# Attention by pairs: scores as three single-pass products of high and low parts, split a query tile at a time inside the stage

## The reference, cut to what matters

```python
# block one: 8 heads, one shared k, the picked keys, causal
logits = jnp.einsum('bthd,btkd->bthk', qb, k_sel).astype(jnp.float32) * (dh ** -0.5)
...
# layers: window_gqa, 6 heads, 2 kv heads, |i - j| <= 128, a sink logit per head
s = jnp.einsum('bnqkgd,bnjkd->bnkgqj', qb, kb).astype(jnp.float32) * (HEAD_DIM ** -0.5)
...
# layers: neighbourhood_attention, 4 heads, a window of 8 x 16 grid cells with a bias table
s = s + bias[None].astype(jnp.float32)
p = jax.nn.softmax(s.reshape(B, NA_HEADS, GRID_W, wh * ww), axis=-1)
```

## Time and profile before

| what | us |
|---|---|
| median of 3 runs | 3905.65 (3900.75 to 3908.73) |
| the profiled execution's own time | 3905.73 |
| its span, first to last instruction | 3903.6 |
| `attend_pairs` in block one | from 437.5 to about 577 |
| `attend_pairs` in the first layer | from 1369.5 to about 1506, neighbourhood pairs from about 1437 |
| `attend_pairs` in the second layer | from about 2736 to 2873 |

### The profile page before, as it was taken

The page is one execution under the profiler, slowest core; times in us unless marked ns, Lnnn a source line. Parts: engine busy times, 40 slices in busy tenths (PEclk is TensorE's granted clock), DMA queues, the critical chain, the costliest instruction groups (busy, mean ns, idle before and its releaser), DMA issues. The chain is left out here.

```text
span 3903.6 us, 54426 instructions
## 1 busy us (share of the span) xinstructions
PE 3484.6 (89%) x18514; PEld 2596.8 (67%) x18514; DVE 2633.7 (67%) x4362; ACT 2047.5 (52%) x3302; POOL 381.4 (10%) x300
## 2 busy tenths in 40 slices
PE   7998989599919999999599999799999995999996
PEld 4444558477718855668488888688556685888884
DVE  1896764588853175664699999631756646999996
ACT  1672451288732165553377777421645532777774
POOL 0002100022141001000011111010010000111110
PEclk9899899699959999999799999899999997999998
DMA  3100002477252110003499999621100034999997
GB/s 115 46 1 3 1 21 100 178 292 296 96 205 73 33 29 23 28 1 125 180 368 393 381 381 383 236 70 33 29 23 28 1 120 181 367 388 382 381 386 275
DMA packets 122029, 649.26 MB, mean 166 GB/s; under 512 B 14064, under 2 KB 22512, under 8 KB 69872
## 3 DMA queue, kind: packets, MB, share of 16 engines
q1 hardware_dynamic: 101392, 572.36, 37.8%
q0 software_dynamic: 15984, 58.20, 5.2%
q10 hardware_dynamic: 4464, 16.25, 1.0%
HBM read 584.38 MB, written 62.39 MB: 166 GB/s over the span
## 5 line engine op out<-in xcount | busy, mean ns | idle before, releaser
L3262 DVE TENSOR_TENSOR low_ring<-mix,high_ring 128x2048 fp32r<-128x2048 f32 x256 | 576.9, 2285 | 41.3 <-ACT high_ring L3211 41.3
L3211 ACT ACTIVATE high_ring<-mix 128x2048 fp32r<-128x2048 f32 x256 | 477.1, 1931 | 80.3 <-PEq L125 80.3
L3150 PE MATMUL ps<-high_ring,x_high 128*128 128x512 f32 x1024 | 408.6, 399 | 10.8 <-DVE low_ring L3262 7.1
L3151 PE MATMUL ps<-low_ring,x_high 128*128 128x512 f32 x1024 | 400.0, 391 | 0.0
L3152 PE MATMUL ps<-high_ring,x_low 128*128 128x512 f32 x1024 | 399.9, 391 | 0.0
L3262 DVE TENSOR_TENSOR low_ring<-more_raw,high_ring 128x2048 fp32r<-128x2048 f32 x128 | 290.3, 2287 | 24.3 <-ACT high_ring L3211 24.3
L3211 ACT ACTIVATE high_ring<-more_raw 128x2048 fp32r<-128x2048 f32 x128 | 246.3, 1924 | 0.0
L3150 PEld LDWEIGHTS ps<-high_ring,x_high 128*128 128x128 f32 x1024 | 192.3, 188 | 73.2 <-DVE low_ring L3262 19.6
L3152 PEld LDWEIGHTS ps<-high_ring,x_low 128*128 128x128 f32 x1024 | 192.3, 188 | 41.0
L3151 PEld LDWEIGHTS ps<-low_ring,x_high 128*128 128x128 f32 x1024 | 192.5, 188 | 37.6
L2717 DVE TENSOR_TENSOR w_unit_low<-mix,w_unit_high 128x1024 fp32r<-128x1024 f32 x32 | 40.9, 1289 | 245.7 <-ACT w_unit_high L2643 245.7
(11 more groups left out here) (495 smaller groups left out, 8124.7 us busy)
## 6 DMA issues: line engine op xcount, KB each, us to landing
mix<-in_expert_units SPq DMA_DIRECT2D x256, 1024.0 KB, 8.0
more_raw<-in_expert_units SPq DMA_DIRECT2D x128, 1024.0 KB, 8.6
raw_experts<-in_expert_units SPq DMA_DIRECT2D x16, 3072.0 KB, 11.5
expert_out<-out ACTq DMA_DIRECT2D x31, 512.0 KB, 2.8
mix<-in_w_turned SPq DMA_DIRECT2D x20, 512.0 KB, 3.7
qk_body<-residual SPq DMA_DIRECT2D x16, 512.0 KB, 8.0
qk_tail<-in_w_out SPq DMA_DIRECT2D x8, 1024.0 KB, 8.3
mix<-residual SPq DMA_DIRECT2D x16, 512.0 KB, 3.3
```

Of the source, the lines that this page charges most:

```text
L3150: nc.tensor.matmul(ps[:, bank, :], left_high, high, start=first, stop=False)
L3151: nc.tensor.matmul(ps[:, bank, :], left_high, low, start=False, stop=False)
L3211: nc.scalar.activation(w_high[:, n % RING, :], raw[n % RAW_UNITS], ACT.Copy).then_inc(high_ready, 1)
L3262: nc.vector.tensor_tensor(w_low[:, n % RING, :], raw[n % RAW_UNITS], w_high[:, n % RING, :].bitcast(F32), ALU.subtract).then_inc(low_ready, 1)
```

## The change

`attend_pairs` gets a list `splits`. An entry is a place (the number of the pair behind which it stands, or -1 for ahead of everything) and a list of parts. For each part ACT copies the raw fp32 operand to an fp32r tile `high`, and DVE subtracts, which gives `low` as fp32r in the place of the raw operand. PE's `score` waits for the step that its pair needs and makes three matmuls per head and unit: high by high, high by low, low by high, the two heads in turn.

In block one there are eight steps, at max(4t - 6, -1) for query tile t: four chunks of q and one of k, 640 columns of 128 rows. In a layer, a tile step at max(3t - 6, -1) holds 256 + 128 columns of q and k and 256 more of the next tile's k (and 256 further ones in the first step; the last has 384 in all), and four more steps of 1024 columns stand behind pairs 4, 8, 12 and 16, for the neighbourhood. So the steps of tiles 0 and 1 stand ahead of everything, and behind pair 12 stand two. The maxima, exponentials, values and transposes are as before. The diff, cut to its core:

```diff
-def attend_pairs(book, ps, ident, pairs, scale, widest, tables=None):
+def attend_pairs(book, ps, ident, pairs, splits, scale, widest, tables=None):
...
-                    for i in range(2):
-                        last = nc.tensor.matmul(ps[:, 2 * (u % 2) + i, 0:cols.stop - cols.start],
-                                                pair["q"][i * HD:(i + 1) * HD, :], pair["k"][i][:, cols],
-                                                start=True, stop=True)
+                    pe.wait_ge(low_made, pair["splits"])
+                    for x, (left, right) in enumerate(((0, 0), (0, 1), (1, 0))):
+                        for i in range(2):
+                            last = nc.tensor.matmul(ps[:, 2 * (u % 2) + i, 0:cols.stop - cols.start],
+                                                    pair["q"][left][i * HD:(i + 1) * HD, :],
+                                                    pair["k"][i][right][:, cols], start=(x == 0), stop=(x == 2),
+                                                    skip_group_check=True)
                     last.then_inc(scores_full, 1)
...
@@ ACT
+            def split(behind):
+                for at, parts in splits:
+                    if at == behind:
+                        for raw, high, _ in parts:
+                            ins = nc.scalar.activation(high, raw, ACT.Copy)
+                        ins.then_inc(high_made, 1)
+
+            split(-1)
             exponentials(0)
             for p in range(N):
...
                 if p + 1 < N:
                     exponentials(p + 1)
+                split(p)
...
@@ DVE
+            def split(behind):
+                for n, (at, parts) in enumerate(splits):
+                    if at == behind:
+                        dve.wait_ge(high_made, n + 1)
+                        for raw, high, low in parts:
+                            ins = nc.vector.tensor_tensor(low, raw, high, ALU.subtract)
+                        ins.then_inc(low_made, 1)
+
+            split(-1)
             maxima(0)
             maxima(1)
...
                 if p >= 2:
                     write(p - 2)
+                split(p)
                 i = p - sums_from
...
@@ block_one
+            splits = [(max(4 * t - 6, -1), [(raw[:, 0:4, tile(t)], high[:, 0:4, tile(t)], raw_low[:, 0:4, tile(t)]),
+                                            (raw[:, 6, tile(t)], high[:, 4, tile(t)], raw_low[:, 6, tile(t)])])
+                      for t in range(T)]
...
@@ layer_two
+                for t in range(T):
+                    of = [(body[:, 4:6, tile(t)], high[:, 4:6, tile(t)], body_low[:, 4:6, tile(t)]),
+                          (tail[:, 0, tile(t)], high[:, 6, tile(t)], tail_low[:, 0, tile(t)])]
+                    for c in ((0, 1) if t == 0 else (t + 1,) if t + 1 < T else ()):
+                        of.append((tail[:, 1:3, tile(c)], high[:, 7:9, tile(c)], tail_low[:, 1:3, tile(c)]))
+                    steps.append((max(3 * t - 6, -1), of, t))
+                for m in range(4):
+                    steps.append((4 + 4 * m, [(body[:, m, :], high[:, m, :], body_low[:, m, :])], T + m))
+                steps = sorted(steps, key=lambda step: step[0])
```

More of the change, by code:

```diff
@@ L3330, in _, with neighbourhood_pairs @@
                 expert(EXPERTS - 1, True, False)
-def neighbourhood_pairs(qk, v, bias, bias_mid, out):
+def neighbourhood_pairs(qk, v, bias, bias_mid, out, splits):
     pairs = []
@@ L3357, in sparse_pairs, with window_pairs @@
         for j in range(HEADS // 2):
-            pairs.append(dict(q=raw[:, j, tile(t)], k=(raw[0:HD, 6, 0:keys], raw[HD:P, 6, 0:keys]), keys=keys,
-                              add=(mask, mask), values=(values, values), out=out[:, t, tile(j)], sink=None))
+            pairs.append(dict(q=[of[:, j, tile(t)] for of in q_parts],
+                              k=([of[0:HD, 0:keys] for of in k_parts], [of[HD:P, 0:keys] for of in k_parts]), keys=keys,
+                              add=(mask, mask), values=(values, values), out=out[:, t, tile(j)], sink=None,
+                              splits=t + 1))
     return pairs
-def window_pairs(qk, v, band, sink, out):
+def window_pairs(qk, v, band, sink, out, splits):
     pairs = []
@@ L3371, in window_pairs @@
             kv = [h // (SWA_HEADS // 2) for h in (2 * j, 2 * j + 1)]
[L3372 removed]
+            pairs.append(dict(q=[of[:, tile(t)] for of in qk[4 + j]],
+                              k=([of[0:HD, keys] for of in qk[7 + kv[0]]], [of[HD:P, keys] for of in qk[7 + kv[1]]]),
                               keys=(hi - lo + 1) * P, add=(add, add),
                               values=[[v[:, c, g * HD:(g + 1) * HD] for c in range(lo, hi + 1)] for g in kv],
[L3375 removed]
+                              out=out[:, t, 640 + j * P:640 + (j + 1) * P], sink=sink[:, 2 * j:2 * j + 2],
+                              splits=splits[t]))
     return pairs
@@ L3511, in layer_two @@
                 sums += [(bias[:, h, GRID_W:], bias[:, h, GRID_W:], outside[:, GRID_W:]) for h in range(NA_HEADS)]
-                window = window_pairs(qk, feats[:, :, 640:768], band, sink, mix)
-                nearest = neighbourhood_pairs(qk, feats[:, :, 0:256], bias, bias_mid, mix)
-                attend_pairs(book, ps, ident, window + nearest, HD ** -0.5, 5 * P, (transfers, sums, len(window)))
+                high = sb(near, "qk_high", [P, 9, S], F32R)
+                low = [body_low[:, m, :] for m in range(MLA_HEADS)] + [tail_low[:, m, :] for m in range(3)]
+                parts = [(high[:, m, :], low[m]) for m in range(9)]
+                steps = []
+                for t in range(T):
[7 more added lines that the diff above has]
+                steps = sorted(steps, key=lambda step: step[0])
+                position = {step[2]: n + 1 for n, step in enumerate(steps)}
+                window = window_pairs(parts, feats[:, :, 640:768], band, sink, mix, position)
+                nearest = neighbourhood_pairs(parts, feats[:, :, 0:256], bias, bias_mid, mix, len(steps))
+                attend_pairs(book, ps, ident, window + nearest, [step[0:2] for step in steps], HD ** -0.5, 5 * P,
+                             (transfers, sums, len(window)))
             with ExitStack() as part:
```

25 lines of the change are left out of this document (19 added, 6 removed).

## The result

| what | before | the change |
|---|---|---|
| median, us | 3908.16 (20 runs, 3900.75 to 3911.97) | 3913.99 (20 runs; 19 of them 3907.27 to 3919.16) |
| ratio, 95% interval | | 1.0018 (1.0012 to 1.0024) |
| profiled execution's own time | 3905.73 | 3914.4 |
| its span | 3903.6 | 3912.6 |
| PE busy, DVE busy | 3484.6, 2633.7 | 3471.3, 2664.1 |

One execution of the change, 5200.85 us at a mean clock of 0.64, was disturbed and is left out of the ratio. The change is slower by 0.18%, some 7.0 us (4.7 to 9.4); the two medians differ by 5.8. The forecast was +11.1 us on 3905.7, so 3917. The sign was right, and so were the stages that lose and gain; the size was some 3 us high against the time and 4 against the ratio.

The account below looks back on a forecast made before the run. PE was taken to bound block one and the neighbourhood, the transposes-copy-exponentials ring and then DVE the window part. Block one -1.5 and two layers at +6.3 gave +11.1 on 3905.7: 3917 us, range 3900 to 3930.

Parts of the forecast that it names:

- Block one: Block one's stage: scores -4.3, start +1.6, later steps +0.5 and clock +0.7, together -1.5 us.
- later steps +0.5: Block one after its start: six splits, one each four pairs, cost 0.5 us for early ones, whose pairs are short.
- Start of a layer: Each layer's start: first splits stand ahead of everything, delaying the start by 2.6 us.
- First stretch: Window part's first stretch: steps add 5.9 us to DVE, some 4.2 free; 1.5 us taken per layer.
- the ring: Window pair: transposes, ACT copy, next pair's exponentials, next transposes; 2.73 us, holding no scores, so shorter scores don't shorten it.
- Second stretch: Window part beside the table sums: steps add 3.7 us to DVE, which sets the pace; 3.4 taken, bounds 1.8 and 3.7.
- Window scores: Layers' window part: scores 2.7 us shorter on PE, nothing taken because of the ring; 2.7 is the other end.
- Pass of 128 keys: 128-key score units: a pass takes 0.11 us, a unit 0.33; rival at floor 0.067, unit 0.20, 3914 us, chance 0.05.
- Clock: Stage starts: longer PE idle and thinner scores cost 0.7 us in block one, 0.5 a layer; ends 0 and 3.5.
- PE as the bound: Rival: PE sets the pace everywhere, DVE's additions are covered, all scores count; 3898 us, with half the effect 3898–3908; chance 0.26.
- The clock's rival: Rival: PE idles more in the window part, so the clock falls or rises later; 3925 to 3945 us, chance 0.13.
- The signs named beforehand: Right: window pairs not shorter, split pairs beside sums over 4 us, DVE never idle; wrong: clock below 1.00 after 10 us.

Follow-up runs that it names:

- the first pair of profiles: One profiled execution each of the kernel before and the change, 3905.73 and 3914.4 us; the second pair repeats both kernels unchanged, 3904.53 and 3913.31 us.
- four steps: Against the change: layers' window pairs multiply raw fp32 with no tile steps, only the four 1024-column splits stay; 3908.51 us, ratio 1.0004 to the kernel before.
- 16 pieces: Against the change: layers' window pairs in fp32, neighbourhood operands split in 16 pieces of 256 columns behind window pairs up to 12; 3905.03 us, ratio 0.9995 to before.
- the best version: Change with layers' window pairs fp32, neighbourhood splits in 256-column pieces, block one's tiles 0 and 1 fp32; 3903.18 us (0.9989 to before), second set 3901.52 (0.9982).
- the splits alone: Against the change: all copies and subtractions made, but PE multiplies raw fp32 operands as before; 3927.75 us, ratio 1.0058 to the kernel before.

## Why the prediction was right, point by point

*Block one* (forecast -1.5). Behind tile 1 the scores gave 4.34 us (forecast 4.3, of which 0.5 were to be paid for later steps; they cost nothing), the first `back` came 1.8 us later (1.6). The first exponential came 1.9 us later. The whole stage is 1.8 shorter in the first pair of profiles and 4.1 in the second. The term "later steps +0.5" was wrong, and the clock term (+0.7) is lost in a scatter of 1.6.

*Start of a layer* (+2.6). The first exponential starts 1.96 us into the second layer's stage before and 4.57 after, +2.61; the first `back` comes 2.2 us later.

*First stretch* (+1.5, and +0.5 for the clock). It was +2.5 at full clock, and this term failed. I set DVE's additions against idle time summed over eight pairs ("some 4.2 are free"). The runs with four steps and with 16 pieces show that it does not add up like that: a step must fit under the ring of its own pair. The excess of a long one is passed on at once. An estimate by this rule, from a turn of 2.34 and a ring of 2.73: a tile step of 0.89 sticks out by 0.50 and one of 1024 columns by 0.75, together 3.0 us for the three and two that lie in the stretch (measured 2.5), and 1.5 for the two of the run with window pairs in fp32 (measured 1.75). The prediction also named only PE's wait at `back` as what a late DVE holds up; ACT's wait at the exponentials was worth 0.9 us.

*Second stretch* (+3.4, ends 1.8 and 3.7). It was +3.0: beside the table sums DVE sets the pace, and nearly all of its 3.56 us more went into the length.

*Window scores* (0, with 2.7 as the other end). Measured at some 0.6 us in the second layer, half of it in the start. *Neighbourhood* (-1.7): -1.95. *Pass of 128 keys*: 0.29 a unit, where I took 0.33 and one of the rivals 0.20.

*Clock* (+0.5 a layer, +0.7 in block one). In a layer's start the half clock did last longer: 13.94 us at 0.63 are 10.3 us of it, against 6.6 before (11.78 at 0.72). Its price depends on what sets the pace. In the first stretch, the first layer took 31.46 us at 0.93 and the second 29.91 at 1.00. Beside the table sums, where DVE sets the pace, 33.02 at 0.95 equals the first layer's 33.01 at 1.00. In block one, where PE does, the same code takes 24.26 us at 0.66, 23.62 at 0.71 and 22.81 at 0.74.

*The sum.* The stages together are 12.3 us longer in the first pair of profiles and 8.5 in the second; the forecast was 11.1. The time grew by 7.0 (4.7 to 9.4). In the first pair the difference lies outside of the stages, in code that no kernel here changes. So it is partly luck that the time came within 3 to 4 us of the forecast: the first stretch was 1 us a layer too low, the second stretch, the neighbourhood and block one's later steps were too high by 0.3 to 0.5 each, and what lies outside was costed at nothing and moved by -3.4 and +0.6 us in the two pairs. The third stretch outside, from the first layer's stage to the second's, in the kernel after and in the second set of the best version:

```profile
1512.81:2737.95 1225.14, 1131.62 (x6000) 890.91 (x6000) 814.63 (x1002) 642.80 (x849) 116.45 (x88) 0.96 0.55 207
```

```profile
1501.77:2735.58 1233.81, 1140.67 (x6000) 899.56 (x6001) 813.83 (x1002) 642.20 (x848) 117.11 (x88) 0.95 0.54 206
```

The same 6000 matmuls are busy 9 us longer at a lower clock, and the stretch is 8.7 us longer. Over everything outside the stages the length was 3485.9 us in the kernel after, 3489.3 in the one before and 3498.3 in the best version, with 421, 437 and 454 us of it at half clock. So the best version's stages were 10 us under those of before and its time only 7.6, and the version without subtractions gained 2 us in the stages and nothing in total. In all twelve kept profiles this outside code took 3485.9 to 3498.3 us, with 421 to 454 us at half clock. The three versions with the shortest stages (405 to 407 us) took 3492 to 3498, but the one with subtractions on POOL, whose stages are among the longest (427), took 3495.6. Whether shorter stages bring about more half clock later, or whether this is scatter, stays open: single profiles can't tell.

*The rivals.* PE as the bound fell with the splits alone. The row halves do overlap. The clock's rival had its mechanism right in part. The layers had 7 to 10 us more at half clock, block one 7 more in the first pair of profiles and none in the second (23.8 us in both kernels). Its price was lower than it said. The argument for it, that the low stretches lie where PE waits most, does not hold for block one: PE is busy 17.99 of 19.80 us there.

*The signs named beforehand.* These came: between `back` 2 and 13 of the second layer no window pair is shorter than 2.86 us, units of 512 keys are 0.18 shorter, and the first exponentials are late as said. These did not: only one pair a layer beside the sums reaches over 4 us (4.21), and DVE still has some 2.3 us of idle time between `back` 8 and 20. One sign of being wrong came: behind the first 10 us of a layer's stage the granted clock was below 1.00, up to about `back` 0 and for 3.4 to 4.2 us more in a later stretch. It cost 1.6 us in the first stretch of the first layer (31.46 against 29.85 once more) and nothing beside the sums.

The Trainium skill (TensorE: Matmul & The Clock Gate, weight-path modes) has a faster weight load for 128 weights that are not FP32. The weight loads of the new scores take 0.19 us in the neighbourhood, as those of the fp32 scores did, so no such gain is seen with fp32r here. The kernel before could have shown it: the weight loads of its fp32r expert weights take 0.19 us too.

## What to carry to other kernels

In this pipeline, work added to an engine that is not the bound was free only in pieces that fit under the ring of one iteration: 4096 columns in 16 pieces cost nothing, 2048 of them in two pieces cost 1.75 us. Don't put the idle time of many iterations against one long step. And don't pay for an operand's preparation where its consumer does not set the pace: the window scores gave some 0.6 us a layer back while their splits cost over 5 (the second layer's stage takes 143.3 us, and 138.5 with window pairs in fp32), whereas the neighbourhood's 2.0 and block one's 4.3 could be had for nothing.

## What the runs showed of the hardware that I had not expected

POOL was no free place for a subtraction beside DVE. One of 1024 columns takes it 2.37 us (DVE: 1.22), and a DVE instruction with two SBUF operands that starts meanwhile ends only after it: 2.60 us instead of 0.82. And with 128 keys the third pass starts 0.11 us behind the second (1487.51 and 1487.62), where 512 keys take 0.23: a quarter of the columns, but half of the time. So short units gain nothing from three single passes: 0.29 us where the fp32 product took 0.22.
